# Front rows issued by SP between weight steps, a middle part for two chunks, two gemv rows in later pairs

## What is computed

```python
def hybrid_layer(x, c_act, g, w_ada, b_ada, w_in, w_out, dec_f, dec_b):
    mod = c_act @ w_ada + b_ada
    shift, scale, gate = jnp.split(mod, 3, axis=-1)
    h = rms_norm(x, g) * (1.0 + scale[:, None]) + shift[:, None]
    proj = jnp.einsum('bsd,df->bsf', h, w_in)
    ... dilated attention and retention on parts of proj ...
    return x + gate[:, None] * out
```

## Time and profile before

| | |
|---|---|
| median of 3 runs | 1435.57 us (1434.3 to 1436.47) |
| the profiled execution | 1434.45 us |
| its span, first to last instruction | 1432.3 us |
| TensorE busy | 1404.6 us, 98% |
| VectorE busy | 1190.1 us, 83% |
| ScalarE busy | 706.8 us, 49% |
| mean DMA rate | 315 GB/s; 416 GB/s in the first 200 us |

### The profile page before, as it was taken

How to read it: one execution, slowest core, us unless ns; L and a number is a source line. 1 busy time by engine, 2 the same in 40 slices (tenths; PEclk the granted TensorE clock), 3 DMA queues, 4 the chain that set the end, 5 groups by cost and what they waited for, 6 DMA issues and landing times.

```text
span 1432.3 us, 19818 instructions
## 1 busy us (share of the span) xinstructions
PE 1404.6 (98%) x6934; PEld 1174.8 (82%) x6934; DVE 1190.1 (83%) x1535; ACT 706.8 (49%) x1041; POOL 143.1 (10%) x235
## 2 busy tenths in 40 slices
PE   7899999999999999999999999999999999999996
PEld 5688888888888788888888888878888888888885
DVE  6899999888998789898878789888797877667566
ACT  6554435654445644444456553364344545465441
POOL 1111110113100000110011100010010001210000
PEclk9999999999999999999999999999999999999999
DMA  9999999988996899999977799689699688775762
GB/s 359 416 416 416 415 410 389 346 311 295 411 402 230 299 339 383 391 395 360 343 224 261 237 331 377 240 301 353 246 359 334 213 304 285 226 248 172 267 193 97
DMA packets 101689, 450.99 MB, mean 315 GB/s; under 512 B 11762, under 2 KB 16226, under 8 KB 77922
## 3 DMA queue, kind: packets, MB, share of 16 engines
q1 hardware_dynamic: 68690, 247.63, 48.5%
q0 software_dynamic: 25616, 185.64, 33.5%
q10 hardware_dynamic: 7296, 16.56, 3.3%
HBM read 447.63 MB, written 2.15 MB: 314 GB/s over the span
## 4 chain that ended last, share of the span: by engine, by line
PE 92%; DMA 3%; DVE 2%; issue 1%; ACT 1%; POOL 0%; DVEq 0%; ACTq 0%
PE bank L907 16%; PE bank L909 16%; PE bank L908 16%; PE bank L890 16%; PE bank L888 8%; PE bank L842 4%; PE bank L844 4%; PE bank L843 4%; DMA raw<-in_t_steps 2%; PE bank L1137 2%; PE bank L1095 2%; PE bank L886 1%; PE bank L855 1%; DVE gw L1694 1%; PE bank L1113 1%
## 5 line engine op out<-in xcount | busy, mean ns | idle before, releaser
L1218 ACT CAST w_hi<-raw 128x1024 fp32r<-128x1024 f32 x436 | 457.2, 1051 | 615.2 <-PE bank L909 309.0
L1666 DVE TENSOR_TENSOR w_lo<-raw,w_hi 128x1024 fp32r<-128x1024 f32 x360 | 437.9, 1224 | 176.5 <-ACT w_hi L1218 175.0
L1694 DVE CUSTOM_DVE_ANT_0 gw<-gw,c_act 128x2048 f32<-128x2048 f32 x176 | 402.0, 2285 | 0.8 <-DMA gw<-in_t_kv_mod 0.3
L908 PE MATMUL bank<-w_lo,act_parts 128*128 128x512 f32 x1024 | 398.8, 389 | 0.0
L907 PE MATMUL bank<-w_hi,act_parts 128*128 128x512 f32 x960 | 386.5, 403 | 0.7 <-issue 0.5
L909 PE MATMUL bank<-w_hi,act_parts 128*128 128x512 f32 x960 | 375.0, 391 | 0.0
L890 PE MATMUL bank<-act_parts,w_hi 128*128 128x512 f32 x960 | 338.3, 395 | 0.0
L888 PE MATMUL bank<-act_parts,w_lo 128*128 128x256 f32 x1024 | 276.9, 281 | 0.0
L908 PEld LDWEIGHTS bank<-w_lo,act_parts 128*128 128x128 f32 x1024 | 192.6, 188 | 38.1
L890 PEld LDWEIGHTS bank<-act_parts,w_hi 128*128 128x128 f32 x960 | 180.1, 188 | 39.1
L909 PEld LDWEIGHTS bank<-w_hi,act_parts 128*128 128x128 f32 x960 | 180.2, 188 | 38.9
(11 more groups left out here) (199 smaller groups left out, 1073.0 us busy)
## 6 DMA issues: line engine op xcount, KB each, us to landing
raw<-in_t_steps SPq DMA_DIRECT2D x464, 512.0 KB, 6.8
gw<-in_t_mod POOLq DMA_DIRECT2D x96, 1024.0 KB, 8.2
gw<-in_t_ada POOLq DMA_DIRECT2D x48, 1024.0 KB, 8.5
gw<-in_t_kv_mod POOLq DMA_DIRECT2D x32, 1024.0 KB, 8.3
area<-gate_rows ACTq DMA_DIRECT2D x3, 1024.0 KB, 10.4
bias<-forget_sums ACTq DMA_DIRECT2D x16, 192.0 KB, 6.7
area<-in_ln_g ACTq DMA_DIRECT2D x2, 1024.0 KB, 7.6
area<-in_ln_b ACTq DMA_DIRECT2D x2, 1024.0 KB, 11.6
```

The lines of the kernel that those rows point to most:

```text
L908: nc.tensor.matmul(dst, hi, w_lo[:, j % SLOTS, k], start=False, stop=False)
L1218: nc.scalar.copy(w_hi[:, b], raw[:, j % SLOTS]).then_inc(hi_ready, 1)
L1666: nc.vector.tensor_tensor(w_lo[:, j % SLOTS], raw[:, j % SLOTS], w_hi[:, j % LEAD].bitcast(F32), ALU.subtract).then_inc(lo_ready, 1)
L1694: nc.vector.tensor_tensor_reduce(out=w, in0=w, in1=c_act[:].rearrange("p (t n) -> p t n", t=TT), scale=1.0, scalar=0.0, op0=ALU.mult, op1= ...
```

## The change

SP issues rows 2 to 31 itself, on its own queue, each right behind the step that `ROW_BEHIND` names; Pool keeps rows 0, 1 and those from 32 on. The waits of SP for row 2 and of Pool for step 2 are gone. SP holds a step back for the low half 6 steps earlier in the first 56 steps instead of 24. `ROW_AT`, `LOW_AT` and `SHIFT_AT` have other turns: row 4 comes in turn 2 instead of 6, row 31 in turn 50 instead of 48. Chunks 8 and 9 get a middle part (k-tiles 4 to 7 and 6 to 7) that is computed in steps 25 to 27, ahead of k-tile 8, and that VectorE adds to the first part in SBUF; chunks 2 to 5 come in the order 3, 5, 4, 2 behind it. Pair 3 takes 6 rows instead of 8, pair 5 takes 11 instead of 10, pair 6 takes 12 instead of 11.

```diff
-PAIR_TILES = {3: 8, 4: 8, 5: 10, 6: 11, 7: 8, 8: 3, 9: 4, 10: 8, 11: 8, 12: 8, 13: 8, 14: 4, 15: 4, 16: 6, 17: 7,
+PAIR_TILES = {3: 6, 4: 8, 5: 11, 6: 12, 7: 8, 8: 3, 9: 4, 10: 8, 11: 8, 12: 8, 13: 8, 14: 4, 15: 4, 16: 6, 17: 7,
...
+MIDDLE = {8: 8, 9: 8}
...
-FRONT += [((q, kt), (q, kt + 1)) for q in (2, 4, 3, 5) for kt in (2, 4, 6)]
+FRONT += [((q, kt), (q, kt + 1)) for q in MIDDLE for kt in range(PARTED[q], MIDDLE[q], 2)]
+FRONT += [((q, kt), (q, kt + 1)) for q in (3, 5, 4, 2) for kt in (2, 4, 6)]
...
-HEAD_LEAD, LEAD_STEPS = 6, 24
+HEAD_LEAD, LEAD_STEPS = 6, 56
...
-ROW_AT = {4: 6, 5: 7, 6: 8, 7: 9, 8: 10, 9: 12, 10: 14, 11: 15, 12: 17, 13: 19, 14: 21, 15: 22}
-ROW_AT.update({g: 24 + int((g - 16) * 1.65) for g in range(16, HEAD_TILES)})
+ROW_AT = {4: 2, 5: 4, 6: 6, 7: 9, 8: 9, 9: 11, 10: 12, 11: 14, 12: 17, 13: 17, 14: 20, 15: 21, 16: 26, 17: 26,
+          18: 27, 19: 31, 20: 32, 21: 33, 22: 35, 23: 36, 24: 37, 25: 41, 26: 43, 27: 43, 28: 45, 29: 46, 30: 49,
+          31: 50}
-LOW_AT = {1: 2, 2: 8, 3: 10, 4: 13, 5: 16, 6: 21, 7: 23}
+LOW_AT = {1: 2, 2: 7, 3: 10, 4: 14, 5: 15, 6: 21, 7: 24, 8: 35, 9: 36, 10: 43, 11: 45, 12: 46, 13: 48, 14: 49,
+          15: 52}
-SHIFT_AT = {1: 2, 2: 9, 3: 10, 4: 14, 5: 18, 6: 22, 7: 25}
+SHIFT_AT = {1: 3, 2: 8, 3: 12, 4: 13, 5: 16, 6: 22, 7: 23, 8: 29, 9: 33, 10: 36, 11: 40, 12: 44, 13: 49, 14: 49,
+            15: 52}
+ROW_BEHIND = {2: 1, 3: 1, 4: 4, 5: 6, 6: 7, 7: 9, 8: 10, 9: 13, 10: 13, 11: 16, 12: 19, 13: 19, 14: 21, 15: 22,
+              16: 23, 17: 27, 18: 28, 19: 33, 20: 34, 21: 34, 22: 35, 23: 37, 24: 37, 25: 42, 26: 43, 27: 44,
+              28: 45, 29: 46, 30: 47, 31: 49}
...
+            def load_row(g):
+                dst, landed, _ = gemv_slot(g)
+                wait(sp, gemv_used, g - GEMV_RING + 1)
+                b, k = mod_at(g)
+                src, row = MOD_SRC[b]
+                sp.dma_start(dst, src[row + k * P:row + (k + 1) * P].rearrange("p (t n) -> p t n", t=TT)
+                             ).then_inc(landed, 16)
...
-                if k == 2:
-
-                    sp.wait_ge(gw_landed[2], 16)
...
                 load_step(k * P, k)
+                for g in range(2, HEAD_TILES):
+                    if ROW_BEHIND[g] == k:
+                        load_row(g)
...
-                if g == C_STORED_WITH:
-                    pool.wait_ge(next_silu, 1)
-                    pool.dma_start(next_silus.rearrange("(k p) -> k p", p=P), next_c).then_inc(c_stored, 16)
...
-            pool.wait_ge(gw_landed[1], 16)
-            for g in range(2, HEAD_TILES + GEMV_RING):
-                if g == 4:
-
-                    pool.wait_ge(raw_landed[2], 16)
+            pool.wait_ge(next_silu, 1)
+            pool.dma_start(next_silus.rearrange("(k p) -> k p", p=P), next_c).then_inc(c_stored, 16)
+            for g in range(HEAD_TILES, HEAD_TILES + GEMV_RING):
                 load(g)
...
+            def merge_part(n):
+
+                for q in closed_at(n, 2):
+                    dve.wait_ge(half_used, n + 1)
+                    dve.wait_ge(parted, TT * (CLOSED[0].index(q) + 1))
+                    for tt in range(TT):
+                        nc.vector.scalar_tensor_tensor(out=part(q, tt), in0=banks[2 * bank_of(q, 2) + tt][:],
+                                                       scalar=part_scale(q), in1=part(q, tt), op0=ALU.mult,
+                                                       op1=ALU.add).then_inc(merged, 1)
...
                     if n >= 0:
+                        merge_part(n)
                         add_part(n)
```

## The result

The changed kernel takes **1444.24 us** in the median (1443.41 to 1444.61), the kernel before 1434.93 beside it: ratio 1.0067, interval 1.0055 to 1.0079, some 9.3 us slower. The forecast was 1438.7 with a range to 1443.0, so the time lies beyond the range. The profiled execution took 1444.16 us with a span of 1442.4, 10.1 more than the span before.

What follows compares the result with a forecast made beforehand. TensorE, busy 98% of the span, was taken as the bound, with DMA and VectorE nearly full in the front. Front -4.0 and pair 5 +7.1 gave +3.1 us: 1438.7 us as a median, range 1433.5 to 1443.

Steps and rivals of the forecast that it cites:

- the front: Weight steps up to step 53: earlier rows on SP's queue were to save 4.0 us, between 3 and 5.
- pair 5: Attention steps: the later c_act fetch and one more row were to cost 7.1 us, bounds 3.6 and 9.6.
- VectorE's stop: In pair 5, VectorE was to stand still 6.3 us before row 48, waiting for the fetch into c_act.
- The chain of half 9 is shifted alike: In pair 5, half 9's chain was to be shifted like half 7's, whose maxima come 7.1 us later.
- the two rows, and what moves with them: Prediction's part on moved rows: row 47 to pair 5's half 1, row 48 to half 2; +7.1 us.
- three waits of 1.3 to 1.9 us: Sign in the front: these TensorE waits gone, with steps 10 and 16 starting earlier than 52.87 and 71.89.
- No wait is due: Front, steps 18 to 53: VectorE needs 88.8 us against TensorE's 95.2, so TensorE was not to wait.
- So nothing for it: Price of SP's queue waiting in order for buffers: nothing, up to 2 us between 20 and 60 us.
- Rival C: The new queue delays the front, early row 4's 3.4 us not won back: front 0, 1442.7 us; chance 0.10.
- step 53 after 173 us: Sign in the front: the prediction is wrong if step 53 starts later than this; about 170 was expected.
- A: Rival in pair 5: c_act's fetch hides, landing within 2.2 us of issue; sum -3.2, 1432.4 us; chance 0.10.
- B: Rival in pair 5: the fetch lands in 4 to 6 us, costing +2.6 to +4.6; about 1435.3 us; chance 0.14.

Runs made afterwards that it cites:

- no_fetch: The changed kernel without the fetch of the second vector into c_act and without the wait for it: 1437.23 us, ratio 1.0016.
- gap_5: The changed kernel with row 48 four halves behind row 47 in pair 5, and pair 6's twelfth row moved to pair 7: 1434.41 us, ratio 0.9997.
- pair6_row: The kernel before with one row moved from pair 7 to pair 6 (11 to 12 and 8 to 7): 1437.68 us, ratio 1.0022.
- pool_30: The changed kernel with the old row counts, and rows 30 and 31 issued by Pool instead of SP: 1436.12 us, ratio 1.001.
- rows_back: The changed kernel with the old row counts (pairs 3, 5, 6 take 8, 10, 11 rows): 1435.13 us, ratio 0.9997.
- row_32_held: The changed kernel with the old row counts, and Pool holding row 32 until row 30 is used instead of row 29: 1435.16 us, ratio 1.0003.
- order_only: The kernel before with only the middle part (front order and merges); rows, their queue and turns as before: 1435.35 us, ratio 1.0004.
- shift_early: The changed kernel with the old row counts, and ScalarE making k-tile 1 in turn 2 instead of 3: 1434.45 us, ratio 1.000.
- three_mends: The changed kernel with old row counts, k-tile 1 on ScalarE in turn 2, row 4 in turn 3, rows 30 and 31 on Pool: 1436.65 us, ratio 1.0015.
- rows_only: The kernel before with only the changed kernel's row counts (pairs 3, 5, 6 take 6, 11, 12): 1444.55 us, ratio 1.0064.
- gap_and_held: The changed kernel with the edits of gap_5 and row 32 held until row 30 is used: 1434.71 us, ratio 1.0002.

## Why the prediction was wrong, and where it was right

The forecast was +3.1 us, and 10.1 came in the span. Of the 7 us between them the front has 3.7, pair 6 has 2.2 and pair 5 has 0.9.

**Pair 5: the mechanism right, the size 0.9 us too small.** VectorE's stop was to be 6.3 us and was 6.40; the landing 277.2 and was 277.3; the maxima of half 7 were to come 7.1 us late and came 7.0, and TensorE's attention step behind them started 7.0 us late. TensorE lost 8.0 in the pair. The step that was short is "The chain of half 9 is shifted alike": half 9's maxima came 9.0 us late, with one of the eleven rows just ahead of them, and TensorE waited 0.75 us for probs_t where it had not waited before. no_fetch and gap_5 have that wait too (0.75 and 0.96 us), so it comes from the eleventh row and not from the fetch. The other 0.3 us are the lead that the front brought and that is lost here as well. The waits were foretold for probs_t alone; 3.0 of the 6.3 us were for qk_t, which stands behind the same work of VectorE.

The landing was met to 0.1 us, and that was partly luck. The same fetch took 8.0 us in the kernel before and 4.7 in pair6_row, which runs the same code up to there; over all versions that have it, it took 4.7 once and 6.9 to 9.1 in the others, 7.6 to 8.6 where it goes out at 267 to 269 us. By the Trainium skill ("DMA: Bandwidth & Descriptors", Anatomy of one DMA — SWDGE (gpsimd) path) it would have been the estimated 4.4; the trace of pair6_row nearly agrees, and the eleven others do not. The DMA engines were busy beside the fast one too (share 0.93 from 252 to 257 us, against 0.97 from 251 to 256 in the kernel before), so what makes the difference is not shown.

**Pair 6: left out.** The diff gives a twelfth row to pair 6, the heading of the prediction's part says "the two rows, and what moves with them", and only pair 5 was worked out. The same arithmetic would have shown it: a row in every half from 1 to 12, and five halves in a row (8 to 12) in which VectorE needs 3.95 us. 2.2 us in the trace, 3.1 in pair6_row.

**The front: -4.0 said, -0.3 there.** This is the largest miss, and it has three parts. (1) Step 3 was to be ready at 32.7 to 34.4 us; it started at 33.46. Right. (2) Step 16 was to start at 68.1 to 69.8 and step 18 at 74 to 76; they started at 70.80 and 76.45. Steps 3 to 16 were to take 35.4 us and took 37.3. The count had TensorE go from step 3 on without a stop; the trace has a wait of 0.94 us before step 10 and one of 0.27 before step 12, and step 10, which was to start earlier than 52.87, started at 53.81. 1.0 to 2.7 us of the miss arise here. (Of the "three waits of 1.3 to 1.9 us" that were to go, one stands before step 0, where the prediction itself says that the change leaves it; the one before step 16 went, and the one before step 10 fell from 1.34 to 0.94.) (3) "No wait is due" from step 18 to 53: right up to step 49, 31 steps in 84.5 us, and wrong behind it, by the 2.0 us before steps 50 and 51. The steps of the prediction that failed are "so no wait is due" and "So nothing for it", its price for SP's queue (its upper end, 2 us, is the size of the waits). It argued that SP had waited 157.2 us with the transfers full all the same. But those waits were for a buffer that TensorE gives back every 2.7 us, and Pool's rows filled the engines meanwhile; now the queue that carries both stands up to 5.7 us before a row, Pool has nothing to issue, and the rate falls to 400 GB/s. The count of megabytes took 416 throughout and compared them with row 31 only: row 31 was to be complete at about 155 us and landed at 158.6, and the steps and row 32 that are wanted next were not counted. How much of the 2.0 us is the queue and how much the transfers as such stays open, since pool_30 freed step 50 from the row ahead of it and kept the waits.

Rival C, the new queue delays the front, had the place (steps behind rows that wait for VectorE) and a time of 1442.7; with pair 6's 2.2 us on top it is near the result. It was given 0.10. Its other half, that the early row 4 is never won back, is not so: at step 49 the front was 2.4 us ahead. By the prediction's own test, step 53 after 173 us, its front was wrong: 174.03. Of A and B, an early landing, A (within 2.2 us) came nowhere near; B (4 to 6 us) came once in twelve fetches, in pair6_row, and not where it counted.

**What stays open.** gap_5 and the changed kernel run the same code in the front, and step 53 stands 152.04 and 153.79 us behind step 0 in their profiled executions. A microsecond or two in the last steps is scatter of single executions, and the old front's spread over 1.0 (153.21 to 154.20), so the gain of the new front is between nothing and about 2 us, and the times (0.9997 for rows_back and for gap_5) can't tell which. Whether VectorE's work or the transfers set steps 50 to 53 was not separated: with row 32 held, VectorE itself stood before that row's bytes. gap_5 made two edits at once, and what each gives is read from no_fetch and pair6_row only. A version with a second buffer for c_act, which would need no distance between rows 47 and 48, was not tried.

## What to carry to other kernels

When rows of work are moved between stages, work out every stage that gets one, the last as well as the first: here one more row cost 2 to 3 us in a stage that had not been looked at. A buffer that is refilled in place needs its distance in time kept when the work around it moves; with its two uses four halves apart instead of one, and the crowded row one pair later, all 9.8 us came back with the same bytes and the same semaphores. And where DMA, VectorE and TensorE are all nearly full, mending one wait can uncover the next one, as row_32_held shows, so single gains are not to be added up to a forecast. Last, slow matmuls ahead of a wait cost nothing if the wait ends when another engine is ready: compare where the wait ends, not how long the matmuls took.

## What the runs showed of the hardware

**The clock after idle time.** TensorE's granted clock fell to its lower level (1.2 GHz) after some idle stretches and not after others of the same length. Before step 2 TensorE idles 2.3 to 3 us in every version. In the changed kernel that was

```profile
28.81 0.76 PE L866 MATMUL bank<-w_hi,act_parts 128*128 128x512 f32 x1 [2.86 <-DVE act_parts L1738]
29.37 0.63 PE L867 MATMUL bank<-w_lo,act_parts 128*128 128x512 f32 x1
```

with matmuls 0.43 us apart instead of 0.227 until 31.5 us. The window from 28 to 32 us had a clock of 0.57 in the changed kernel, rows_back and order_only, 0.71 to 0.82 in shift_early, pool_30 and three_mends, and 1.00 in the kernel before, rows_only, pair6_row, no_fetch, gap_5, gap_and_held and row_32_held. no_fetch and gap_5 have the changed kernel's order of work there, so it is not the order of work that decides it, and nothing here shows what does. What the lower clock costs depends on what comes next. In the changed kernel it cost little at step 3, which VectorE sets in any case (13.22 us behind step 0 with the drop, 12.60 to 13.05 in versions of this front without it). In order_only, where step 3 stands behind no row, step 3 started at 12.38 us instead of 10.86, and by step 16 all but 0.3 us of that was made up. In pair 5 of the changed kernel the drop behind the stop of 2.56 us cost nothing, and the stop of 2.96 us after it was followed by full clock. In rows_only it was the other way round: full clock behind 1.54 us of idle time, and 0.50 from 292 to 296 us behind 4.59. There it did cost: TensorE reached its next attention step 6.54 us after 291.70, where the changed kernel took 4.42 us for the same work, while what that step needed from ScalarE had been ready at 296.0.

**Landing times in full engines.** Steps of half a megabyte that SP issued from 130 to 155 us, in the kernel before (no rows on SP's queue) and in the changed one:

```profile
L648 SPq DMA_DIRECT2D raw<-in_t_steps x10: 328/328/328, 130.1 to 154.6; - x10
...
DMA to landing us min/median/max: 12.1/13.8/15.5
```

```profile
L666 SPq DMA_DIRECT2D raw<-in_t_steps x10: 327/382/723, 130.9 to 154.7; - x10
...
DMA to landing us min/median/max: 8.2/10.6/14.1
```

The time from issue to landing tells little by itself: the steps of the kernel before went out earlier and stayed outstanding longer. Half a megabyte issued 0.4 us behind a megabyte on the same queue landed 12.4 us after its issue, the megabyte itself 9.1 us, and a megabyte on Pool's queue at the same time 9.1. In the front of the kernel that is more than four steps of TensorE, and one and the same fetch of a megabyte took 8.0 us in one execution and 4.7 in another.
